# A mixture-of-experts layer in fp32: the third matrix of each expert is loaded from GpSimd's DMA queue instead of SP's

## The chip, the cores and the metric

The kernel runs on one NeuronCore of a Trainium2 chip. The metric is the time of one execution on the device in microseconds. PE is TensorE (matmuls), ACT is ScalarE, DVE is VectorE, POOL is GpSimd, SP is SyncE, which here does nothing but issue DMAs. SP, ACT and GpSimd each have a DMA queue of their own; in the profile q1 is SP's, q10 ACT's and q0 GpSimd's. All of them run on the same 16 DMA engines.

## The reference

The whole is one block of a first model (two sequence branches of a Hyena convolution and an mLSTM, merged, then an expert layer) and two layers of a second model (attention, retention, gated feed-forward), on 256 tokens of 1024 channels, all in fp32. What the change touches is the expert layer. Sixteen experts each pick their 32 best tokens (`cap` = 2 x 256 / 16) and send them through three matrices:

```python
def expert_choice_ffn(h, w_router, w1, w3, w2):
    B, N, D = h.shape
    cap = EC_CAPACITY_FACTOR * N // N_EXPERTS
    aff = jax.nn.softmax((h @ w_router).astype(jnp.float32), axis=-1)
    gate, idx = lax.top_k(jnp.swapaxes(aff, 1, 2), cap)
    bidx = jnp.arange(B)[:, None, None]
    xg = h[bidx, idx]
    a = jnp.einsum('becd,edf->becf', xg, w1)
    b = jnp.einsum('becd,edf->becf', xg, w3)
    ye = jnp.einsum('becf,efd->becd', jax.nn.silu(a) * b, w2) * gate[..., None].astype(h.dtype)
    return jnp.zeros_like(h).at[bidx, idx].add(ye)
```

`w1` and `w3` are 1024 x 2048 for each expert and `w2` is 2048 x 1024, 8 MiB each: 24 MiB per expert and 384 MiB for all. Every weight is used once.

## The kernel before

The program is written by hand, engine by engine, with semaphores. Nothing is scheduled by a tool: what an engine does, and in which order, is the order of its code.

**Chunks and slots.** Each matrix of an expert is loaded in four chunks of 2 MiB, [128 partitions x 16 KiB], and each partition's 16 KiB are contiguous in memory. An expert has `PER_EXPERT` = 12 chunks, in the order of use: c0 to c3 are w1, c4 to c7 are w3, c8 to c11 are w2 (`E1`, `E3`, `E2` in the code). The chunks of all experts go through `XRING` = 8 slots, four in the tile `ring_sb` and four in `arena_sb`: chunk number n of the whole stage lies in slot n mod 8. So eight chunks, two thirds of an expert, are in memory or in flight at a time.

**Who waits for what.** PE adds one to the semaphore `slots_used` with the last matmul on each chunk. The load of chunk n waits until chunk n - 8 has been used, and that is its only wait. Each slot has a semaphore `expert_landed[slot]`; PE waits for it before a chunk (`slot_of`). In the kernel before, SP issues all loads in the order of use: expert 0's first eight chunks are loaded ahead, while the branches before are at work, then a loop over pairs of experts issues 24 loads per turn (L645), and a last part 16 more (L649). After these come, on the same queue, the weights of the next two layers in half chunks of 1 MiB (`halves`, L659); the first four of them go to slots 2, 3, 5 and 6 of the eight and wait for the last expert's c6, c7, c9 and c10 to be used.

**What PE does for an expert** (`expert`, L2065): eight chunks of 16 matmul records, into two banks; after c3 it spreads the next expert's gates; after c7 it turns the gates and the product of the first two matrices (`hact`, which DVE makes once c7 is used), gathers the next expert's tokens by a one-hot product (8 us), and then does c8 to c11 with the turned `hact` (`hTs`, which DVE copies out of PSUM). At the end ACT copies the result and PE scatters it to all tokens; DVE adds it up. The last expert has no gather for a next one.

**GpSimd** has some loads of constants to issue at the beginning, one store, and four loads of small tables at about 310 us (L720). Then it has nothing to do until the two layers after the experts, where it makes the low part of each half chunk (L725).

Of the kernel before, what the change touches and what calls it, by code (L numbers as in the profile page):

```python
# [32 lines left out]
XRING = 8  # L33
# [11 lines left out]
EXPERTS, CAP, FF = 16, 32, 2048  # L45
# [176 lines left out]
def kernel_program(nc, a, k, out):  # L222
# [3 lines left out]
    with ExitStack() as ctx:  # L226
# [3 lines left out]
        def sem(name):  # L230
            return ctx.enter_context(nc.semaphore(name))
# [26 lines left out]
        def region(off, *dims):  # L258
            n = int(np.prod(dims))
            v = arena[:, off:off + n]  # L260
            if len(dims) == 2:
                return v.rearrange("p (a b) -> p a b", a=dims[0])
            if len(dims) == 3:
                return v.rearrange("p (a b c) -> p a b c", a=dims[0], b=dims[1])
            if len(dims) == 4:
                return v.rearrange("p (a b c d) -> p a b c d", a=dims[0], b=dims[1], c=dims[2])
            return v
# [113 lines left out]
        rows = arena[0:4, 4096:4096 + 3136]  # L381
# [19 lines left out]
        def spread_row(ap, off, n):  # L401

            return bass.AP(ap.tensor, off, [[0, P], [1, n]])
# [37 lines left out]
        s = {n: sem(n) for n in names}  # L441
        landed = [sem(f"slot{i}_landed") for i in range(RING)]
        expert_landed = [sem(f"expert{i}_landed") for i in range(XRING)]
        half_landed = [sem(f"half{i}_landed") for i in range(RING)]


# [49 lines left out]
        E1 = a["w_exp1"][0].rearrange("e (p k) f -> e p k f", p=P)  # L496
        E3 = a["w_exp3"][0].rearrange("e (p k) f -> e p k f", p=P)
        E2 = a["w_exp2"][0].rearrange("e (r p c) f -> e r p c f", p=P, c=4)
        PER_EXPERT = 12
        N_POST = N_PRE + PER_EXPERT * EXPERTS  # L500
        def expert_slot(c, *dims):

            i = c % XRING
            if i in EXPERT_ARENA:
                v = region(EXPERT_ARENA[i], SLOT)
            else:
                o = ((N_PRE + EXPERT_RING.index(i)) % RING) * SLOT
                v = ring[:, o:o + SLOT]
            return v.rearrange("p (k c) -> p k c", k=dims[0])
# [23 lines left out]
        for l in range(DEPTH_2):  # L533
# [28 lines left out]
            for i in range(NF // 2):  # L562
                src = a["w_ffn_down_2"][l][2 * P * i:2 * P * (i + 1)].rearrange("(k p) c -> p k c", p=P)
# [6 lines left out]
        def half(n, t=ring):  # L570

            o, (kk, c) = ((N_POST + n) % RING) * SLOT, halves[n][1]
            return tuple(t[:, b:b + kk * c].rearrange("p (k c) -> p k c", k=kk) for b in (o, o + HALF))
# [12 lines left out]
        def wait_emptied(eng, name, n=None):  # L586
# [9 lines left out]
            for e, v in last.items():  # L596
                eng.wait_ge(freed[e], v)

        block = ctx.enter_context(nc.Block())


        @block.sync
        def _(sp):
# [19 lines left out]
            def expert_load(e, c, place=None):  # L623

                place = c if place is None else place
                n = 2 if c < 8 else 4
                src = E2[e, c - 8] if c >= 8 else (E1, E3)[c // 4][e, :, 2 * (c % 4):2 * (c % 4) + 2]
                sp.dma_start(expert_slot(place, n), src).then_inc(expert_landed[place % XRING], 16)

            expert_load(0, 0)  # L630
            sp.wait_ge(s["unit_done"], U.at("yo1", 1) + 1)
# [11 lines left out]
            expert_load(0, 7)  # L643

            with sp.Fori(0, EXPERTS - 2, 2) as e:  # L645
                for c in range(XRING, XRING + 2 * PER_EXPERT):
                    sp.wait_ge(s["slots_used"], e * PER_EXPERT + (c - XRING + 1))
                    expert_load(e + c // PER_EXPERT, c % PER_EXPERT, c)
            for c in range(XRING, 2 * PER_EXPERT):  # L649
                sp.wait_ge(s["slots_used"], (EXPERTS - 2) * PER_EXPERT + c - XRING + 1)  # L650
                expert_load(EXPERTS - 2 + c // PER_EXPERT, c % PER_EXPERT, c)
            for n, (src, _, _, _) in enumerate(halves):
# [8 lines left out]
                for l in range(DEPTH_2):  # L661
                    i = n - half_at["va", l] - RING
# [6 lines left out]
                    if 1 <= i <= 3:  # L669

                        h = HPG * (i - 1)
                        src = bass.AP(rel_table.tensor, 127 + h * P * 384, [[383, P], [P * 384, HPG], [1, T]])
                        sp.dma_start(relB[:, h:h + HPG], src).then_inc(s["lay_landed"], 16)
                    if i == 4:
                        src = bass.AP(a["b_in_2"].tensor, l * IN2 + V_R, [[0, P], [0, 2], [1, 2048]])
# [21 lines left out]
        @block.gpsimd  # L697
        def _(pool):
            g = nc.gpsimd
            g.memset(sTad, 0.0)  # L700
            g.memset(ones[:], 1.0)
            g.memset(cst[:, 0:1], EPS)
            g.memset(cst[:, 1:2], 1.0).then_inc(s["cst_set"], 1)
            g.memset(cst[:, 2:3], LN_EPS).then_inc(s["cst_set"], 1)
            for dst, src in other_loads:
                g.dma_start(dst, src).then_inc(s["small_landed"], 16)

            pool.wait_ge(s["unit_done"], U.at("filt", 7) + 1)
            g.memset(vx[:, :, :, 128:129], 1.0)
            g.memset(vc[:, :, :, 128:129], 1.0).then_inc(s["vaug_ones"], 1)  # L710

            pool.wait_ge(s["rel_ready"], 1)

            g.dma_start(rel_table, relbuf.unsqueeze(1).broadcast_to([AH, P, 384])).then_inc(s["rel_saved"], 16)

            pool.wait_ge(s["unit_done"], U.at("hT", 1) + 1)
            for dst, src in ((ltmask.rearrange("p t s -> p (t s)"), k["ltmask"]), (iota, k["iota"]),
                             (w_router, a["w_router"][0].rearrange("(p k) c -> p k c", p=P)),
                             (fnorm, spread_row(a["final_norm_g"], 0, D))):
                g.dma_start(dst, src).then_inc(s["moe_landed"], 16)  # L720

            for n in range(len(halves)):
                pool.wait_ge(s["hi_ready"], n + 1)
                low, high = half(n, ring_r)
                g.tensor_tensor(low, half(n)[0], high.bitcast(F32), ALU.subtract).then_inc(s["lo_ready"], 1)  # L725
# [1018 lines left out]
        def _(pe):  # L1744
# [63 lines left out]
            for i in range(8):  # L1808
                t, c = divmod(i, 4)
# [30 lines left out]
            for i in range(8):  # L1840
                o, f, q = i // 4, (i // 2) % 2, i % 2
# [70 lines left out]
            for d in range(2):  # L1912
                for t in range(2):
                    c = (d * 2 + t) * 4
# [30 lines left out]
            for kind, r in enumerate((3, 0, 2)):  # L1945
                for d in range(2):
                    for t in range(2):
                        c = kind * 16 + (d * 2 + t) * 4
# [34 lines left out]
            for o in range(2):  # L1983
# [17 lines left out]
                for i in range(2):  # L2001
                    b = open_unit(f"yo{o}", i)
                    for j in range(2):
                        n = 0
# [60 lines left out]
            def expert(e, pair, second, last=False):  # L2065
                def slot_of(c, n):
                    place = PER_EXPERT * second + c
                    pe.wait_ge(expert_landed[place % XRING], 16 * (place // XRING + 1) + pair * (16 * PER_EXPERT // XRING))
                    return expert_slot(place, n)
                pe.wait_ge(s["xg_copied"], e + 1)  # L2070
                for c in range(8):
                    w = slot_of(c, 2)
                    o = bank[c // 4]
                    for q in range(2):
                        kt_ = 2 * (c % 4) + q
                        for g in range(4):
                            ins = mm(o[32 * g:32 * g + 32, :], xg[:, kt_], w[:, q, 512 * g:512 * g + 512], kt_ == 0, kt_ == 7)
                    ins.then_inc(s["slots_used"], 1)
                    if c == 3 and not last:
                        spread_gates(e + 1)  # L2080
                pe.wait_ge(s["sg_copied"], e + 1)
                if not last:
                    pe.wait_ge(s["sel_ready"], e + 2)
                for t in range(2):
                    ins = tr(bank[3][:, t * P:(t + 1) * P], sgs[:, t])
                ins.then_inc(s["sg_turned"], 1)
                pe.wait_ge(s["hact"], e + 1)
                for c in range(4):
                    ins = tr(bank[2][:, c * P:(c + 1) * P], hact[:, c:512:4])
                ins.then_inc(s["hT_turned"], 1)  # L2090
                if not last:
                    gather(e + 1)
                pe.wait_ge(s["hT_evac"], e + 1)
                for r in range(4):
                    w = slot_of(8 + r, 4)
                    for c in range(4):
                        for g in range(4):
                            ins = mm(bank[0][32 * g:32 * g + 32, 0:T], hTs[:, c, 32 * r:32 * r + 32], w[:, c, T * g:T * (g + 1)],
                                     r + c == 0, r + c == 6)
                    ins.then_inc(s["slots_used"], 1)  # L2100

                pe.wait_ge(s["y_evac"], e + 1)
                pe.wait_ge(s["sgT_evac"], e + 1)
                pe.wait_ge(s["acc_done"], e + 1)
                for t in range(2):
                    for g in range(4):
                        ins = mm(bank[4 + g][:, t * T:(t + 1) * T], sgT[32 * g:32 * g + 32, t * P:(t + 1) * P], ysb[32 * g:32 * g + 32])
                ins.then_inc(s["scat_done"], 1)
# [105 lines left out]
            for l in range(DEPTH_2):  # L2214
# [99 lines left out]
                n = half_at["mixo", l]  # L2314
# [154 lines left out]
```

## Time and profile before

| | |
|---|---|
| median of 3 runs | 2553.28 us (2551.95 to 2556.81) |
| the profiled execution | 2555.6 us, its span 2553.8 us |
| mean granted clock of TensorE | 0.906 of full speed |
| PE busy | 2209.2 us, 87% of the span |
| DVE, ACT, GpSimd busy | 725.6, 648.6, 859.1 us |
| DMA | 679.90 MB, mean 266 GB/s |
| loads of expert weights | 192 of 2048 KB, 35.6 us from issue to landing |
| chain that ended last | PE 64%, DMA 29% |

The span is the time that the trace covers, the profiled execution's own time has some us around it, and the median is that of runs without a profile. The shares are means over stages with different limits: the expert stage lies at 447 to 1360 us, and its limit has to be read there. The 35.6 us from issue to landing are no latency, since each load queues behind those issued before it.

### The profile page before, as it was taken

What the parts mean: (1) busy time and instruction counts of PE and PEld (TensorE: products, weight loads), DVE (VectorE), ACT (ScalarE), POOL (GpSimd) and SP (SyncE); (2) the same over time, 40 slices, a digit from 0 to 9 for tenths busy, and PEclk for the clock granted to TensorE, in tenths of its full rate; (3) what the DMA queues carried; (4) which work ended last, traced back from release to release, by engine and by line L of the source; (5) the groups of instructions that cost most, each with busy time, mean ns of one, the idle gap of its engine ahead of it and who ended that gap; (6) DMA issues with size and microseconds to landing.
All of it is one profiled execution on the core that took longest, in us unless ns stands there. A gap on an engine that the chain in (4) does not pass through costs nothing.

```text
span 2553.8 us, 30814 instructions
## 1 busy us (share of the span) xinstructions
PE 2209.2 (87%) x13012; PEld 1553.4 (61%) x13012; DVE 725.6 (28%) x1446; ACT 648.6 (25%) x786; POOL 859.1 (34%) x212
## 2 busy tenths in 40 slices
PE   6999998867777676776666999999999999999998
PEld 2678775323333322222224887887887888888887
DVE  4233433111111111111114152643322152644231
ACT  1211300000000000000002443644443443553442
POOL 1000000000000000000004765777887855677786
PEclk9999997787777878778787999999999999999999
DMA  9456324999999999999996744465655744456563
GB/s 342 128 190 238 113 99 197 389 428 428 429 428 428 429 428 429 429 428 429 428 426 234 241 135 130 149 181 190 207 196 166 259 148 133 132 174 198 185 194 132
DMA packets 236692, 679.90 MB, mean 266 GB/s; under 512 B 8748, under 2 KB 153142, under 8 KB 211313
## 3 DMA queue, kind: packets, MB, share of 16 engines
q1 hardware_dynamic: 233905, 671.54, 69.4%
q0 software_dynamic: 2400, 6.41, 1.0%
q8 instruction: 74, 1.21, 0.2%
q10 hardware_dynamic: 288, 0.53, 0.1%
q14 instruction: 25, 0.20, 0.0%
HBM read 673.85 MB, written 4.59 MB: 266 GB/s over the span
## 4 chain that ended last, share of the span: by engine, by line
PE 64%; DMA 29%; DVE 4%; ACT 1%; issue 1%; POOL 1%; SPq 0%; DVEq 0%; ACTq 0%
PE bank L1759 63%; DMA arena_sb<-w_exp 24%; DMA ring_sb<-w_exp 4%; PE bank L1762 2%; DVE arena_sb L1046 1%; DVE bank L1049 1%; POOL ring_parts L725 1%; DVE x_sb L1049 0%; DMA arena_sb<-hy_skip 0%; ACT ring_parts L911 0%; DVE sm_sb L1530 0%; DVE bank L1046 0%; ACT arena_sb L935 0%; SPq L615 0%; DVE arena_sb L1049 0%
## 5 line engine op out<-in xcount | busy, mean ns | idle before, releaser
L725 POOL TENSOR_TENSOR ring_parts<-ring_sb,ring_parts 128x2048 fp32r<-128x2048 f32 x186 | 848.4, 4578 | 1374.5 <-ACT ring_parts L911 1374.1
L1759 PE MATMUL bank<-arena_sb 128*32 128x256 f32 (+8 forms) x3550 | 562.0, 544 | 148.7 <-DMA arena_sb<-w_exp 112.7
L1759 PEld LDWEIGHTS bank<-arena_sb 128*32 128x32 f32 (+4 forms) x3550 | 318.5, 181 | 358.4 <-DMA arena_sb<-w_exp 154.6
L1759 PE MATMUL bank<-arena_parts,ring_parts 128*128 128x256 f32 (+1 forms) x2288 | 425.9, 334 | 0.0
L1759 PE MATMUL bank<-ring_sb,arena_sb 128*32 128x512 f32 (+2 forms) x2336 | 303.4, 610 | 134.8 <-DMA ring_sb<-w_exp 134.8
L911 ACT CAST ring_parts<-ring_sb 128x2048 fp32r<-128x2048 f32 x186 | 349.7, 1886 | 191.4 <-DMA ring_sb<-w_in 61.2
L1759 PEld LDWEIGHTS bank<-arena_parts,ring_parts 128*128 128x128 f32 x2288 | 359.3, 188 | 48.4
L1046 DVE TENSOR_TENSOR arena_sb<-bank,arena_sb 128x512 f32<-128x512 f32 (+5 forms) x245 | 145.1, 611 | 797.0 <-PE bank L1759 689.4
L1759 PE MATMUL bank<-hT_parts,ring_parts 128*128 128x256 f32 (+1 forms) x1632 | 323.0, 340 | 0.3 <-POOL ring_parts L725 0.3
L1759 PEld LDWEIGHTS bank<-ring_sb,arena_sb 128*32 128x32 f32 (+1 forms) x2336 | 89.1, 126 | 340.8 <-DMA ring_sb<-w_exp 215.4
L1759 PEld LDWEIGHTS bank<-hT_parts,ring_parts 128*128 128x128 f32 x1632 | 262.1, 189 | 38.6 <-issue 1.9
L1759 PE MATMUL bank<-ring_parts,arena_parts 128*128 128x512 f32 (+1 forms) x1152 | 262.3, 385 | 0.0
L1759 PEld LDWEIGHTS bank<-ring_parts,arena_parts 128*128 128x128 f32 x1152 | 212.7, 188 | 42.7
L1046 DVE TENSOR_TENSOR bank<-bank,arena_sb 128x256 f32<-128x256 f32 (+1 forms) x250 | 124.7, 502 | 323.7 <-ACT arena_sb L935 304.3
L901 ACT COPY arena_sb<-bank 128x256 f32<-128x256 f32 x16 | 6.0, 372 | 594.8 <-PE bank L1759 594.8
L1759 PE MATMUL bank<-hT_sb,ring_sb 128*128 128x256 f32 x640 | 142.4, 383 | 0.0
L1759 PEld LDWEIGHTS bank<-hT_sb,ring_sb 128*128 128x128 f32 x640 | 122.2, 192 | 19.6 <-issue 3.1
L1759 PE MATMUL bank<-ring_parts,hT_parts 128*128 128x512 f32 (+1 forms) x432 | 101.6, 390 | 8.6 <-DVE hT_parts L1046 5.1
L1759 PEld LDWEIGHTS bank<-ring_parts,hT_parts 128*128 128x128 f32 x432 | 79.8, 195 | 26.3 <-DVE hT_parts L1046 5.9
L935 ACT ACTIVATE arena_sb<-bank,colC_sb 128x256 f32<-128x256 f32 x132 | 61.9, 473 | 133.5 <-PE bank L1759 133.4
L899 ACT ACTIVATE arena_sb<-bank 128x512 f32<-128x512 f32 x16 | 9.6, 597 | 296.7 <-PE bank L1759 296.7
L1762 PEld LDWEIGHTS bank<-ident_sb,arena_sb 128*128 128x128 f32 x426 | 54.5, 162 | 49.0 <-issue 22.5
(213 smaller groups left out, 1011.0 us busy)
## 6 DMA issues: line engine op xcount, KB each, us to landing
arena_sb<-w_exp SPq DMA_DIRECT2D x96, 2048.0 KB, 35.6
ring_sb<-w_exp SPq DMA_DIRECT2D x96, 2048.0 KB, 35.6
ring_sb<-w_in SPq DMA_DIRECT2D x112, 1024.0 KB, 5.4
ring_sb<-w_ada SPq DMA_DIRECT2D x24, 1024.0 KB, 12.4
ring_sb<-w_ffn_gate SPq DMA_DIRECT2D x22, 1024.0 KB, 5.3
ring_sb<-w_ffn_up SPq DMA_DIRECT2D x22, 1024.0 KB, 5.3
ring_sb<-w_ffn_down SPq DMA_DIRECT2D x22, 1024.0 KB, 4.9
ring_sb<-w_ret_proj SPq DMA_DIRECT2D x16, 1024.0 KB, 5.8
```

The source lines that it names most:

```text
L725: g.tensor_tensor(low, half(n)[0], high.bitcast(F32), ALU.subtract).then_inc(s["lo_ready"], 1)
L899: A.activation(sact, bank[0][:], ACT.Silu).then_inc(s["a_read"], 1)
L901: A.copy(ysb, bank[0][:, 0:T]).then_inc(s["y_evac"], 1)
L911: A.copy(half(n, ring_r)[1], half(n)[0]).then_inc(s["hi_ready"], 1)
L935: A.activation(spare[:, n % 3], bank[u % 8][:, T:2 * T], ACT.Identity, bias=0.0 if c is None else colC[:, c + j:c + j + 1]).then_inc(s["sp ...
L1046: return V.tensor_tensor(o, i0, i1, op)
L1049: return V.scalar_tensor_tensor(o, i0, sc, i1, op0, op1)
L1759: return M.matmul(o, l, r, start=first, stop=last)
L1762: return M.transpose(o, i, ident[:])
```

## The change

The loads of c8 to c11 are issued from GpSimd's queue, in a loop of its own of the same form, with the same waits for `slots_used`. SP's loop leaves these chunks out. Since two queues now fill the same slots, there is a second set of landing semaphores, `rows_landed`, for GpSimd's loads, and PE waits for one or the other; a place of the ring holds a chunk of the third matrix once in a pair of experts. Expert 0's first eight chunks, none of them of the third matrix, are loaded by SP as before. Nothing in the work of PE, ACT or DVE changes.

```diff
+        rows_landed = [sem(f"rows{i}_landed") for i in range(XRING)]
...
+        def first_columns(c0, c1):
+            return [c for c in range(c0, c1) if c % PER_EXPERT < 8]
+        def second_rows(c0, c1):
+            return [c for c in range(c0, c1) if c % PER_EXPERT >= 8]
+        def expert_source(e, c):
+            return E2[e, c - 8] if c >= 8 else (E1, E3)[c // 4][e, :, 2 * (c % 4):2 * (c % 4) + 2]
...
             with sp.Fori(0, EXPERTS - 2, 2) as e:
-                for c in range(XRING, XRING + 2 * PER_EXPERT):
+                for c in first_columns(XRING, XRING + 2 * PER_EXPERT):
                     sp.wait_ge(s["slots_used"], e * PER_EXPERT + (c - XRING + 1))
                     expert_load(e + c // PER_EXPERT, c % PER_EXPERT, c)
-            for c in range(XRING, 2 * PER_EXPERT):
+            for c in first_columns(XRING, 2 * PER_EXPERT):
...
+            def second_load(e, c, place):
+                g.dma_start(expert_slot(place, 4), expert_source(e, c)).then_inc(rows_landed[place % XRING], 16)
+            with pool.Fori(0, EXPERTS - 2, 2) as e:
+                for c in second_rows(XRING, XRING + 2 * PER_EXPERT):
+                    pool.wait_ge(s["slots_used"], e * PER_EXPERT + (c - XRING + 1))
+                    second_load(e + c // PER_EXPERT, c % PER_EXPERT, c)
+            for c in second_rows(XRING, 2 * PER_EXPERT):
+                pool.wait_ge(s["slots_used"], (EXPERTS - 2) * PER_EXPERT + c - XRING + 1)
+                second_load(EXPERTS - 2 + c // PER_EXPERT, c % PER_EXPERT, c)
...
                 def slot_of(c, n):
                     place = PER_EXPERT * second + c
-                    pe.wait_ge(expert_landed[place % XRING], 16 * (place // XRING + 1) + pair * (16 * PER_EXPERT // XRING))
+                    if c >= 8:
+                        pe.wait_ge(rows_landed[place % XRING], 16 + 8 * pair)
+                    else:
+                        uses = len([p for p in first_columns(0, place + 1) if p % XRING == place % XRING])
+                        pe.wait_ge(expert_landed[place % XRING], 16 * uses + 16 * pair)
```

On GpSimd's engine, from the four table loads to its first work for the next layer, before:

```order
L720 DMA arena_sb<-const_ltmask 128x512 [waits unit_done]
L720 DMA arena_sb<-const_iota 128x32
L720 DMA arena_sb<-w_router 128x128
L720 DMA arena_sb<-final_norm_g 128x1024
L725 ISA
L725 TENSOR_TENSOR ring_parts<-ring_sb,ring_parts 128x2048 [waits hi_ready] x4
```

and now, from the last two of the table loads to the second load of the loop:

```order
L731 DMA arena_sb<-w_router 128x128
L731 DMA arena_sb<-final_norm_g 128x1024
L737 UNCONDITIONAL_BRANCH
L737 ISA
L735 ISA [waits slots_used]
L735 DMA arena_sb<-w_exp 128x4096
L739 REGISTER_ALU
L735 ISA [waits slots_used]
L735 DMA arena_sb<-w_exp 128x4096
L739 REGISTER_ALU
```

Eight loads stand in the loop (two are shown) and eight more behind it; line numbers are 11 to 27 higher than before. The loop also has a wait (ISA) and a register step at each load. On SP's queue, the beginning of the loop, before, where the first four loads are those of the third matrix (slots 0 to 3, two in `arena_sb` and two in `ring_sb`):

```order
L628 ISA [waits slots_used]
L628 DMA arena_sb<-w_exp 128x4096
L647 REGISTER_ALU
L628 ISA [waits slots_used]
L628 DMA arena_sb<-w_exp 128x4096
L647 REGISTER_ALU
L628 ISA [waits slots_used]
L628 DMA ring_sb<-w_exp 128x4096
L647 REGISTER_ALU
L628 ISA [waits slots_used]
L628 DMA ring_sb<-w_exp 128x4096
L647 REGISTER_ALU
```

and now, where the same place has the next expert's c0 to c2 (slots 4 to 6):

```order
L639 ISA [waits slots_used]
L639 DMA arena_sb<-w_exp 128x4096
L658 REGISTER_ALU
L639 ISA [waits slots_used]
L639 DMA ring_sb<-w_exp 128x4096
L658 REGISTER_ALU
L639 ISA [waits slots_used]
L639 DMA ring_sb<-w_exp 128x4096
```

SP's loop starts with the next expert's c0, which waits for this expert's c4 to be used; c8 to c11 of this expert, which wait for c0 to c3, are no longer ahead of it.

## Rows read from the trace of the kernel before

**Rows 1.** The page, part 2: 40 equal slices of the span, tenths busy and GB/s.

```profile
DMA  9456324999999999999996744465655744456563
GB/s 342 128 190 238 113 99 197 389 428 428 429 428 428 429 428 429 429 428 429 428 426 234 241 135 130 149 181 190 207 196 166 259 148 133 132 174 198 185 194 132
```

**Rows 2.** Table of stretches: the stage of the expert loads.

```profile
core 0: us, PE busy (x) PEld busy (x) DVE busy (x) ACT busy (x) POOL busy (x), PEclk, DMA share, GB/s
500.00:1300.00 800.00, 569.84 (x4290) 249.70 (x4286) 105.71 (x297) 29.65 (x40) 0.00 (x0) 0.77 1.01 428
```

**Rows 3.** DMA queues, 500 to 1300 us: GB/s in 40 slices, packets, then the queue.

```profile
GB/s 427 426 429 430 425 429 430 428 427 430 429 425 430 430 426 428 431 427 427 432 426 427 432 428 425 431 429 426 430 430 426 428 431 426 428 432 428 425 430 428
DMA packets 23530, 342.68 MB, mean 428 GB/s; under 512 B 2615, under 2 KB 2615, under 8 KB 2615
...
q1 hardware_dynamic: 23526, 342.62, 100.6%
```

**Rows 4.** Waits of PE, 500 to 1300 us: total, times, longest.

```profile
PE bank L1759 <- DMA ring_sb<-w_exp: 120.9, 57, 3.0
PE bank L1759 <- DMA arena_sb<-w_exp: 97.6, 57, 3.0
```

**Rows 5.** Timeline of PE, last expert: start, length, engine, line, tiles.

```profile
1307.14 3.61 PE L1759 MATMUL bank<-ring_sb,arena_sb 128*32 128x512 f32 x16 [2.87 <-DMA ring_sb<-w_exp]
1312.03 1.92 PE L1759 MATMUL bank<-ring_sb,arena_sb 128*32 128x512 f32 x16 [1.29 <-DMA ring_sb<-w_exp]
...
1351.19 3.35 PE L1759 MATMUL bank<-ring_sb,arena_sb 128*32 128x256 f32 x32 [2.96 <-DMA ring_sb<-w_exp]
1356.10 1.93 PE L1759 MATMUL bank<-arena_sb 128*32 128x256 f32 x32 [1.56 <-DMA arena_sb<-w_exp]
```

**Rows 6.** Timeline of SP's queue, first load of the loop.

```profile
451.13 2.02 SPq L628 DMA_DIRECT2D arena_sb<-w_exp  x2
```

**Rows 7.** Chain that ended last, 400 to 1400 us: start, length, what.

```profile
1320.17 35.88 DMA arena_sb<-w_exp
```

**Rows 8.** Waits of SP, 500 to 1300 us.

```profile
SPq L628 <- PE bank L1759: 714.6, 164, 12.3
```

**Rows 9.** Timeline of GpSimd, the first of four loads in a row.

```profile
309.71 0.56 POOL L720 DMA_DIRECT2D arena_sb<-const_ltmask  x1 [233.18 <-PE bank L1762]
```

**Rows 10.** DMA issues, whole program: count, KB each, us to landing.

```profile
ring_sb<-w_in SPq DMA_DIRECT2D x112, 1024.0 KB, 5.4
...
arena_sb<-final_norm_g POOLq DMA_DIRECT2D x1, 512.0 KB, 8.7
```

**Rows 11.** DMA queues, 315 to 317 us.

```profile
q0 software_dynamic: 136, 0.37, 53.4%
q1 hardware_dynamic: 163, 0.33, 46.4%
```

**Rows 12.** Timeline of all engines, the middle of one expert.

```profile
749.08 1.92 PE L1759 MATMUL bank<-ring_sb,arena_sb 128*32 128x512 f32 x16 [1.41 <-DMA ring_sb<-w_exp]
...
752.40 11.27 PE L1759 MATMUL bank<-arena_sb 128*128 128x32 f32 x64
752.60 0.69 DVE L1476 COPY arena_sb<-bank 128x512 f32<-128x512 f32 x1
760.13 0.43 DVE L1046 TENSOR_TENSOR arena_sb<-bank,gcol_sb 128x256 f32<-128x256 f32 x1 [6.84 <-PE bank L1759]
...
763.44 4.13 PE L1759 MATMUL bank<-ring_sb,arena_sb 128*32 128x256 f32 x64
```

**Rows 13.** Timeline of SP's queue, first loads of the next layer.

```profile
1335.00 20.14 SPq L659 DMA_DIRECT2D ring_sb<-w_in  x4
```

**Rows 14.** Timeline of ACT, its first cast for the next layer.

```profile
1368.72 3.69 ACT L911 CAST ring_parts<-ring_sb 128x2048 fp32r<-128x2048 f32 x2
```

**Rows 15.** Table of stretches: SP's queue alone, then both queues.

```profile
311.50:313.50 2.00, 2.00 (x5) 0.90 (x6) 0.00 (x0) 0.00 (x0) 0.35 (x1) 1.00 1.05 409
314.50:317.50 3.00, 3.00 (x9) 1.33 (x8) 2.27 (x4) 0.00 (x0) 0.00 (x0) 1.00 1.06 376
```

More of the change, by code:

```diff
@@ L625, in expert_load @@
                 place = c if place is None else place
-                n = 2 if c < 8 else 4
-                src = E2[e, c - 8] if c >= 8 else (E1, E3)[c // 4][e, :, 2 * (c % 4):2 * (c % 4) + 2]
-                sp.dma_start(expert_slot(place, n), src).then_inc(expert_landed[place % XRING], 16)
+                sp.dma_start(expert_slot(place, 2), expert_source(e, c)).then_inc(expert_landed[place % XRING], 16)
             expert_load(0, 0)
```

## The prediction, made before the changed kernel ran

> **What bounds the kernel now.** I read the page's 40 slices first. From slice 8 to slice 20 the DMA line stands at 9 and moves 426 to 429 GB/s, beside 100 to 260 in most of the program after it [rows 1]. The table of stretches puts numbers to it: from 500 to 1300 us the 16 DMA engines are busy for 1.01 of the time at 428 GB/s, PE for 570 of 800 us, at a granted clock of 0.77 of full speed, so partly at 1.2 and partly at 2.4 GHz; GpSimd does nothing [rows 2]. The DMA rows say that all of this is one queue, q1 (SP's), in packets that come to 16.4 KB each: 342.6 MB over 23530 - 2615 packets [rows 3]. The waits agree: PE waits 120.9 + 97.6 us for expert weights there [rows 4]. The timeline shows the step: weight matmuls start at 1307.14 and 1312.03 [rows 5], so one 2 MiB chunk every 4.89 us, and an expert of 12 chunks takes 58.7 us. From SP's first load of the loop at 451.13 [rows 6] to the last chunk's landing at 1356.05 (1320.17 + 35.88 in the chain [rows 7]) are 905 us for 184 chunks. The time of this stage is bytes over rate. PE's order changes it only if it lets the DMA engines run dry, or in what is left to do after the last chunk.
>
> **What the change moves.** I number an expert's chunks c0 to c11; c8 to c11 are its third matrix. All 64 of these loads leave SP's queue for GpSimd's; slots, slot waits, bytes and PE's order stay. What follows:
>
> 1. Issuing. SP has 64 issues fewer, which is worth nothing: it spends 714.6 us of 800 waiting for PE to use a slot [rows 8]. GpSimd gets 64 issues of 0.56 us or so each [rows 9], some 36 us in a stage in which it is idle and nobody waits for it; its loop is over before its first work for the next layer. Cost 0. A transfer may start later: a 512 KB load on this queue took 8.7 us to land, beside a busy SP queue, where SP's 1 MiB loads have a median of 5.4 [rows 10]. But a chunk's slot is freed 8 x 4.89 = 39 us before its use, so a few us are hidden as long as something else is in flight. Cost 0 as well.
>
> 2. The order of arrival. With one queue chunks land in the order of use. With two, c8 starts as soon as its slot is free instead of behind seven others. In the stretch where both queues have something to carry, 315 to 317 us, q0 moved 0.37 MB and q1 0.33 MB in 136 and 163 packets [rows 11]: about half each. So I let both share the rate equally. Then per expert: c8 to c11 are released as c0 to c3 are used, and take 4 x 9.8 = 39 us; SP brings four chunks in the same time, 9.8 us each, and then four more alone in 19.6 us. Sum 58.7 us, as before.
>
> 3. Do the engines run dry? The danger is after c7. PE then turns hact, gathers the next expert's tokens and only then starts c8: c7 ends at 751.0, the gather runs from 752.4 to 760.1, which is 9.1 us after c7, and c8 is done at 763.4 [rows 12]. Before, c10 and c11 still land in that time. Now c8 to c11 are there, and what is in flight are the four chunks c0 to c3 of the next expert, 19.6 us of transfers, against some 12 us until the first slot comes free. 7 us to spare: the rate holds. Cost 0, but this is where the cover can go (see the starvation below).
>
> 4. The tail. Before, the last thing to land is c11 at 1356.05, and behind it stand only its matmuls, 1.93 us, to 1358.03 [rows 5]. Now the third matrix comes early and c7 late. The last bytes still land at 1356 (same bytes, rate and start), shared by c7 and c11; c7's slot was freed earlier, so it lands up to one half-rate chunk before them, at 1346 to 1356. I take 1349. Behind it stand its matmuls (2.7 us, the mean of the two lengths in the timeline, 1.9 and 3.5), the chain to c8 (from c7's end at 751.00 to the end of DVE's copy of the turned hact at 753.29: 2.3 [rows 12]; the last expert has no gather), and four chunks of the third matrix back to back (10.8): 1349 + 15.8 = 1364.8, 6.8 us later than 1358.03. Ends: c7 at 1346 and PE at 2.4 GHz (1.9 + 2.3 + 7.7) gives 1358, or 0; c7 last of all and PE at 1.2 GHz (3.6 + 2.3 + 14) gives 1376, or +18. I take +8, as a PE that has waited for c7 may be at the lower level. The four half chunks of the next layer, issued from 1335 on [rows 13] and needed by ACT at 1368.7 [rows 14], ride behind c7 instead of behind c11 and are not late. The rest of the program only shifts.
>
> 5. The rate with two queues. The trace has no expert load on GpSimd's queue, so this is bounded from neighbours. q1 alone, 311.5 to 313.5 us: 409 GB/s. Both queues, 314.5 to 317.5 us: 376 GB/s [rows 15], 8% less, with small packets. Both queues would be active for 2/3 of the 905 us (39 of 58.7), 603 us. Upper end, the same ratio, 409/376 = 1.088: +53 us. If the loss is a fixed one per packet instead, it shrinks with size: a mean packet there is 0.70 MB/299 = 2.3 KB, here 16.4 KB, so 0.088 x 2.3/16.4 = 1.2%, or +7 us. Lower end: two full slices of the stage stand at 429 against a mean of 428 [rows 1], and within it finer slices at 432 [rows 3]; a second queue that fills gaps all the time could give 1%, -8 us. I take the per-packet reading, +7 us, since the stretch it comes from is the nearest row there is and the packets are what differs most.
>
> Sum on the profiled execution, 2555.6 us: 8 + 7 more are 2570.6. The runs' median is 2.3 us lower, 2553.28, so 2568.
>
> The Trainium skill (DMA: Bandwidth & Descriptors, "Issuing engines are not separate DMA queues") says that spreading DMAs over issuing engines saves only issue time. The trace agrees as far as SP's issue time is free; by this rule step 5 would be 0 and the result 2561.
>
> **Rivals.**
> *Starvation of GpSimd's queue.* If its packets are small and the engines alternate packet by packet, it gets far less than half while SP has work: with packets of 4 KB against 16.4, one fifth. For it: nothing in the trace shows a large packet from this queue. Against it: bytes came out even at 315 to 317 us, though the packets differed in number [rows 11]. Then c10 and c11 land last, with SP's next eight chunks but one already in their slots, and the engines have nothing to carry in two gaps: while PE does c11 and SP starts the load it admits (2.7 + 1.4), and, when that has landed, until PE has closed the expert and done the next c0 and GpSimd's first load starts (2.5 + 2.7 + 4, less 4.9 for the one chunk). The 1.4 and 4 are my estimates from the landings in [rows 10], less the transfers. About 8 us per expert over 15 experts: +117, with the tail 2680; partly so, 2590 to 2640.
> The Trainium skill (same page, "Queues, rings and completion order" and "SWDGE vs HWDGE vs iDMA") has engines going round the queues a packet at a time, and GpSimd's packets preferably at most 4096 bytes: read literally this is that case. The trace bears it out only in part, for the bytes were even.
> *The mixed rate is 8% lower* for large packets too: 2553 + 53 + 8 = 2614. For it the one mixed stretch; against it that its packets are small, and that some engines may have had nothing left to do.
> *Hidden anyway, no change.* The tail is at its lower end (c7 early, PE at 2.4 GHz) and the rate stays: 2553 to 2558.
> *Faster.* Two queues leave fewer gaps, 432 GB/s for 428: -8, with a tail of +2: 2547.
>
> **Chances.** Forecast (equal shares, tail, small loss) 0.50, mostly 2559 to 2580; lower mixed rate 0.13; starvation 0.10; no change 0.17; faster 0.10. The runs tell a change from none at about 0.2%, 5 us. So slower 0.73, same 0.17, faster 0.10. The range reaches from within the faster case, 2548, to just over the lower mixed rate, 2618, and leaves out the full starvation.
>
> **What would show it.** Step 2: in the DMA rows of the stage q0 has a third of the bytes; PE's waits are for the expert's c4 to c7, with some 9.8 us between their starts, and c8 to c11 run without any. Step 3: the DMA line stays at 9 in every slice; an 8, or PE waiting for the third matrix, means starvation. Step 4: behind the last c7 stand four back-to-back chunks, and the last scatter comes 6 to 10 us after the last landing. Step 5: 424 to 426 GB/s from 500 to 900 us by the forecast, 404 by the proportional loss, 432 by the gain. The forecast is wrong if the 905 us of the stage change by more than 15, or if anything after the experts changes by more than 3.

## The result and the profile after

The changed kernel takes 2561.63 us (median of 7 runs, 2559.89 to 2565.55) against 2553.47 us before (7 runs): a ratio of 1.0034, 95% interval 1.0024 to 1.0044, so 8 us slower, between 6 and 11. The profiled execution's span is 2561.0 us, 7.2 us longer than before. The forecast was 2568, made of +8 for the tail (what PE still has to do behind its last wait for a weight) and +7 for the rate with two queues. The sign and the mechanism of the tail were right; the rate did not change at all.

Part 2 of the page of the changed kernel, the same 40 slices (PE busy, granted clock, DMA busy, GB/s):

```profile
PE   6999998766666767666666999999999999999998
...
PEclk9999997777777677677777999999999999999999
DMA  9456324999999999999995844455655844356553
GB/s 338 130 192 236 112 99 197 381 427 429 427 429 429 428 429 428 428 429 428 428 427 195 270 132 132 143 178 181 217 187 171 260 142 147 117 181 203 184 195 132
```

The DMA line holds 9 from slice 8 to 20, at 427 to 429 GB/s, as in [rows 1]. The stretch from 500 to 1300 us, in the columns of [rows 2], and its DMA rows:

```profile
500.00:1300.00 800.00, 529.01 (x4158) 241.74 (x4150) 106.21 (x301) 29.87 (x40) 28.75 (x55) 0.72 1.01 428
```

```profile
DMA packets 23515, 342.64 MB, mean 428 GB/s; under 512 B 2602, under 2 KB 2602, under 8 KB 2602
...
q1 hardware_dynamic: 15528, 226.20, 66.4%
q0 software_dynamic: 7983, 116.38, 34.2%
```

428 GB/s and a share of 1.01, the same as before [rows 2, 3], though a third of the bytes now comes through q0. The packets are as large as before: (342.64 MB) / (23515 - 2602) = 16.4 KB. (The 2602 packets under 512 B, 16 for each load, hold 4 bytes each; they count as packets in the rows below too.) PE is at a lower mean clock, 0.72 for 0.77. The waits of PE in this stretch:

```profile
PE bank L1782 <- DMA ring_sb<-w_exp: 178.2, 28, 7.9
PE bank L1782 <- DMA arena_sb<-w_exp: 82.4, 15, 7.0
```

260.6 us in 43 waits, where [rows 4] has 218.5 in 114: fewer and longer ones. The timeline of PE in the middle of an expert (start, length, as in [rows 5]) shows which:

```profile
745.23 3.17 PE L1782 MATMUL bank<-arena_sb 128*32 128x512 f32 x16 [4.42 <-DMA arena_sb<-w_exp]
755.02 3.64 PE L1782 MATMUL bank<-ring_sb,arena_sb 128*32 128x512 f32 x16 [6.62 <-DMA ring_sb<-w_exp]
764.81 3.64 PE L1782 MATMUL bank<-ring_sb,arena_sb 128*32 128x512 f32 x16 [6.16 <-DMA ring_sb<-w_exp]
...
769.95 11.28 PE L1782 MATMUL bank<-arena_sb 128*128 128x32 f32 x64
780.99 4.78 PE L1782 MATMUL bank<-ring_sb,arena_sb 128*32 128x256 f32 x64
785.60 1.90 PE L1782 MATMUL bank<-arena_sb 128*32 128x256 f32 x32
```

The last three chunks before the gather start at 745.23, 755.02 and 764.81, 9.8 us apart instead of 4.89 [rows 5], each after 4 to 7 us of waiting; then come the gather and, without a wait for DMA, c8 to c11 (records at 769.95, 780.99 and 785.60). This is step 2 of the prediction as forecast, but for c4: it starts at 738.88 without a wait, where the prediction had waits for c4 to c7. GpSimd's own rows, its loads for expert 0 and the first of the next four, and the landing times from part 6 of the page:

```profile
453.45 0.53 POOL L735 DMA_DIRECT2D arena_sb<-w_exp  x1 [139.73 <-PE bank L1782]
...
498.00 0.53 POOL L735 DMA_DIRECT2D arena_sb<-w_exp  x1 [38.92 <-PE bank L1782]
```

```profile
arena_sb<-w_exp POOLq DMA_DIRECT2D x32, 2048.0 KB, 14.6
ring_sb<-w_exp POOLq DMA_DIRECT2D x32, 2048.0 KB, 30.2
```

Each issue takes 0.53 us, and between groups of four GpSimd is idle for 39 to 56 us. The four loads of a group are issued within some 5 us and land one after the other, so the medians of 14.6 and 30.2 us are places in that row. Now the end of the stage, the last expert on PE:

```profile
1345.43 3.64 PE L1782 MATMUL bank<-ring_sb,arena_sb 128*32 128x512 f32 x16 [6.15 <-DMA ring_sb<-w_exp]
1355.20 3.64 PE L1782 MATMUL bank<-ring_sb,arena_sb 128*32 128x512 f32 x16 [6.14 <-DMA ring_sb<-w_exp]
...
1359.66 0.89 PE L1785 MATMUL bank<-ident_sb,arena_sb 128*128 128x128 f32 x4 [0.20 <-DVE arena_sb L1069]
1361.33 1.93 PE L1782 MATMUL bank<-arena_sb 128*32 128x256 f32 x32 [0.78 <-DVE arena_sb L1499]
1363.08 3.64 PE L1782 MATMUL bank<-ring_sb,arena_sb 128*32 128x256 f32 x64
1366.54 1.91 PE L1782 MATMUL bank<-arena_sb 128*32 128x256 f32 x32
1368.94 1.15 PE L1782 MATMUL bank<-arena_sb 32*128 32x256 f32 x16 [0.49 <-ACT arena_sb L924]
```

c6 starts at 1345.43 and c7 at 1355.20, and each of them had been waited for 6.1 us. In [rows 5] the last record of this kind that waits is c11 at 1356.10, followed by nothing but the scatter, in the trace of before:

```profile
1358.53 1.15 PE L1759 MATMUL bank<-arena_sb 32*128 32x256 f32 x16 [0.49 <-ACT arena_sb L901]
```

In the changed kernel the scatter starts at 1368.94: behind the landing of c7 stand its own matmuls, 3.64 us, the turned `hact` until 1360.55, its copy, and the four chunks of w2 from 1361.33 to 1368.45. c7 is not the last chunk to land. GpSimd's load of c11, issued at 1323.75, has this row (DMA issues of 1323 to 1324.5 us, the last number from issue to landing):

```profile
arena_sb<-w_exp POOLq DMA_DIRECT2D x1, 2048.0 KB, 35.1
```

It lands at 1358.85, 3.7 us after c7, and nobody waits for it, since PE comes to it at 1366.54. From the first load of the loop, GpSimd's at 453.45, to this landing are 905.4 us, as before. So all the bytes arrive in the same time, and what costs is that the last chunk that PE has to wait for now has four others behind it. The granted clock of the two parts (columns of [rows 2]):

```profile
1355.00:1359.00 4.00, 3.79 (x17) 0.82 (x18) 0.09 (x1) 0.00 (x0) 0.00 (x0) 0.50 0.94 376
1361.00:1369.00 8.00, 7.17 (x132) 4.12 (x132) 5.08 (x5) 0.47 (x2) 0.00 (x0) 1.00 0.65 227
```

c7 runs at 0.50, the level of 1.2 GHz, after PE has waited 6.1 us for it; the four chunks of w2 run at 1.00, that of 2.4 GHz.

### The profile page after: what moved, and what is told of

It reads as the page before. It is cut to its first block, busy times and chain, and to the rows that moved or that the text cites. A ratio compares the mean times of both kernels' runs of the same rounds, so it can differ in the third digit from the quotient of the medians.

```text
span 2561.0 us, 30831 instructions
## 1 busy us (share of the span) xinstructions
PE 2177.8 (85%) x13012; PEld 1553.8 (61%) x13012; DVE 725.5 (28%) x1446; ACT 648.5 (25%) x786; POOL 892.7 (35%) x276
## 4 chain that ended last, share of the span: by engine, by line
PE 69%; DMA 23%; DVE 4%; ACT 1%; issue 1%; POOL 1%; SPq 0%; DVEq 0%; POOLq 0%; ACTq 0%
PE bank L1782 67%; DMA ring_sb<-w_exp 13%; DMA arena_sb<-w_exp 10%; PE bank L1785 2%; DVE arena_sb L1069 1%; POOL ring_parts L748 1%; DVE bank L1072 1%; ACT ring_parts L934 0%; DVE x_sb L1072 0%; DMA arena_sb<-hy_skip 0%; DVE sm_sb L1553 0%; DVE bank L1069 0%; DMA ring_sb<-w_ffn_gate 0%; DVE arena_sb L1072 0%; ACT arena_sb L958 0%
## 5 line engine op out<-in xcount | busy, mean ns | idle before, releaser
L1782 PE MATMUL bank<-arena_sb 128*32 128x256 f32 (+8 forms) x3550 | 541.1, 520 | 126.5 <-DMA arena_sb<-w_exp 91.1
L735 POOL DMA_DIRECT2D arena_sb<-w_exp x32 | 16.9, 528 | 938.8 <-PE bank L1782 938.8
## 6 DMA issues: line engine op xcount, KB each, us to landing
arena_sb<-w_exp POOLq DMA_DIRECT2D x32, 2048.0 KB, 14.6
ring_sb<-w_exp POOLq DMA_DIRECT2D x32, 2048.0 KB, 30.2
```

The lines of the kernel that those rows point to most:

```text
L735: g.dma_start(expert_slot(place, 4), expert_source(e, c)).then_inc(rows_landed[place % XRING], 16)
L1782: return M.matmul(o, l, r, start=first, stop=last)
```

## The experiments

The table gives, for each profiled execution, the first matmul on an expert chunk, the first work of GpSimd for the next layer, what lies between them (the stage), and the rest of the span. Everything is read from the timelines of PE and GpSimd. Each ratio is against runs of the kernel before beside it; e5 and e6 ran on another chip than e1 to e4 (medians of before: 2554.50 and 2552.94 us).

| kernel | first matmul | first low part | stage, us | against before | rest of the span | ratio of the runs (95%) |
|---|---|---|---|---|---|---|
| before | 447.58 | 1370.69 | 923.1 | | 1630.7 | |
| changed | 449.45 | 1381.10 | 931.7 | +8.5 | 1629.3 | 1.0034 (1.0024 to 1.0044) |
| e1, last expert back on SP | 450.62 | 1374.20 | 923.6 | +0.5 | 1628.0 | 0.9999 (0.9989 to 1.0009) |
| e2, last expert alone on GpSimd | 448.75 | 1382.47 | 933.7 | +10.6 | 1630.4 | 1.0038 (1.0023 to 1.0052) |
| e3, w1 on GpSimd instead of w2 | 451.07 | 1374.53 | 923.5 | +0.4 | 1629.3 | 1.0005 (0.9994 to 1.0015) |
| e4, 4 KB packets on GpSimd's queue | 448.42 | 1433.73 | 985.3 | +62.2 | 1625.8 | 1.0215 (1.0198 to 1.0233) |
| e5, 4 KB packets for w2, all on SP | 449.63 | 1389.78 | 940.2 | +17.0 | 1627.2 | 1.0066 (1.0045 to 1.0087) |
| e6, 4 KB packets on both queues | 451.01 | 1421.68 | 970.7 | +47.6 | 1632.8 | 1.0204 (1.0187 to 1.0221) |

The rest of the span varies over 7 us among the eight executions, without following any edit that I can name (no edit touches the kernel behind the stage); what the edits do is in the stage.

**e1: the last expert's third matrix back on SP.** Four of the 64 loads are returned.

```diff
-            for c in first_columns(XRING, 2 * PER_EXPERT):
+            for c in first_columns(XRING, 2 * PER_EXPERT) + second_rows(PER_EXPERT, 2 * PER_EXPERT):
...
-            for c in second_rows(XRING, 2 * PER_EXPERT):
+            for c in second_rows(XRING, PER_EXPERT):
...
-                    if c >= 8:
+                    if c >= 8 and last:
+                        pe.wait_ge(expert_landed[place % XRING], 48 + 16 * pair)
+                    elif c >= 8:
```

> The changed kernel, but the third matrix of the last expert (four of the 64 loads) is back on SP's queue, in the order of use. Tail theory: all of the +8 us comes from the last expert, where four chunks' matmuls now stand behind the last landing instead of one; with c8 to c11 last again, the time is that of before, 2553 +- 2 (ratio 0.999 to 1.001), and the span from the last landing to the last scatter is 4 us as before, not 14. Rival, a cost spread over the stage (rate with two queues, start of loads, PE's lower clock): 15 of 16 experts still use both queues, so 15/16 of the loss stays, 2561 (ratio 1.003).

Measured: 2554.07 us, ratio 0.9999. The loss is gone, with 15 of 16 experts still on two queues. The timeline of PE at the end of the stage (c7, c10, c11, scatter):

```profile
1340.02 2.79 PE L1782 MATMUL bank<-ring_sb,arena_sb 128*32 128x512 f32 x16 [2.98 <-DMA ring_sb<-w_exp]
...
1354.69 3.54 PE L1782 MATMUL bank<-ring_sb,arena_sb 128*32 128x256 f32 x32 [2.96 <-DMA ring_sb<-w_exp]
1359.60 1.93 PE L1782 MATMUL bank<-arena_sb 128*32 128x256 f32 x32 [1.36 <-DMA arena_sb<-w_exp]
1362.03 1.15 PE L1782 MATMUL bank<-arena_sb 32*128 32x256 f32 x16 [0.49 <-ACT arena_sb L924]
```

c7 is done at 1342.81, 17 us before c11's matmuls start, and c11 is again the last to be waited for. The rival of a cost spread over the stage falls: it had 1.003, and the interval ends at 1.0009.

**e2: only the last expert's third matrix on GpSimd's queue**, in the kernel before.

```diff
-            for c in range(XRING, 2 * PER_EXPERT):
+            for c in range(XRING, 2 * PER_EXPERT - 4):
...
+            for c in range(2 * PER_EXPERT - 4, 2 * PER_EXPERT):
+                pool.wait_ge(s["slots_used"], (EXPERTS - 2) * PER_EXPERT + c - XRING + 1)
+                g.dma_start(expert_slot(c, 4), E2[EXPERTS - 1, c % PER_EXPERT - 8]).then_inc(rows_landed[c % XRING], 16)
```

> The kernel before, but the third matrix of the last expert alone (four loads) is issued from GpSimd's queue. Tail theory: the whole loss appears with these four loads, 2561 to 2562 (ratio 1.003 to 1.004), the last expert's c4 to c7 start 9.8 us apart and all other experts' chunks 4.9. Rival of a spread cost: 1/16 of the loss, under 1 us, 2553 to 2554.

Measured: ratio 1.0038, so four loads of 192 make the whole loss, and the stage is longer by 10.6 us. PE in the last expert:

```profile
1336.22 3.48 PE L1764 MATMUL bank<-arena_sb 128*32 128x512 f32 x16 [6.54 <-DMA arena_sb<-w_exp]
1346.02 3.64 PE L1764 MATMUL bank<-arena_sb 128*32 128x512 f32 x16 [6.32 <-DMA arena_sb<-w_exp]
...
1357.01 3.32 PE L1764 MATMUL bank<-ring_sb,arena_sb 128*32 128x512 f32 x16 [2.09 <-DMA ring_sb<-w_exp]
...
1362.69 1.93 PE L1764 MATMUL bank<-arena_sb 128*32 128x256 f32 x32 [0.79 <-DVE arena_sb L1481]
1364.44 3.64 PE L1764 MATMUL bank<-ring_sb,arena_sb 128*32 128x256 f32 x64
1367.90 1.91 PE L1764 MATMUL bank<-arena_sb 128*32 128x256 f32 x32
1370.30 1.15 PE L1764 MATMUL bank<-arena_sb 32*128 32x256 f32 x16 [0.49 <-ACT arena_sb L906]
```

Chunks 9.8 us apart at 1336.22 and 1346.02, one landing last before 1357.01, and behind it the three records of w2 and the scatter at 1370.30. (The expectation had c4 to c7 all 9.8 us apart. c2 to c5 are, and the last two follow at 6 and 5 us: with one queue until then, c0 to c3 are used one by one, GpSimd's four loads go out from 1305.5 to 1330.0, and the last of them lands at 1349.4 (19.4 us after its issue), before c6 and c7 have come. So here c7 lands last of all, at 1357.0, where in the changed kernel it came 3.7 us before the last landing; that makes these four loads alone cost 2 us more than all 64.)

**e3: the first matrix on GpSimd's queue instead of the third.** c0 to c3 of all experts, expert 0's too, are issued by GpSimd and c4 to c11 by SP.

```diff
         def first_columns(c0, c1):
-            return [c for c in range(c0, c1) if c % PER_EXPERT < 8]
+            return [c for c in range(c0, c1) if c % PER_EXPERT >= 4]
         def second_rows(c0, c1):
-            return [c for c in range(c0, c1) if c % PER_EXPERT >= 8]
+            return [c for c in range(c0, c1) if c % PER_EXPERT < 4]
```

> The same split, a third of each expert on GpSimd's queue, but it is the first half of the first two matrices' chunks in order of use, c0 to c3 (w1), that GpSimd loads, for all experts, and SP loads c4 to c11. Tail theory: in the last expert c0 to c3 come early and c11 lands last, so one chunk's matmuls stand behind the last landing as before: 2553 +- 3. Two queues are active for as long as in the changed kernel, so a rival that lays the loss on the second queue itself expects 2561. A third outcome, over 2565, would mean that c8 to c11 at half rate arrive too late for PE and slots stay full: the DMA rate in the stage would be below 428 GB/s.

Measured: 2554.7 us, ratio 1.0005. Both queues carry about as much as in the changed kernel (q0 has 114.43 MB from 500 to 1300 us, for 116.38), at 428 GB/s, and nothing is lost. c10 and c11 on PE:

```profile
1355.04 3.57 PE L1784 MATMUL bank<-ring_sb,arena_sb 128*32 128x256 f32 x32 [2.96 <-DMA ring_sb<-w_exp]
1359.94 1.93 PE L1784 MATMUL bank<-arena_sb 128*32 128x256 f32 x32 [1.33 <-DMA arena_sb<-w_exp]
```

c11 is the last that PE waits for, and one chunk's matmuls stand behind it. What costs is which chunk PE waits for last, not the second queue.

**e4: small packets on GpSimd's queue.** This asks what the prediction's starvation rival hangs on: how the DMA engines share between the queues.

```diff
-                g.dma_start(expert_slot(place, 4), expert_source(e, c)).then_inc(rows_landed[place % XRING], 16)
+                for h in range(2):
+                    g.dma_start(expert_slot(place, 4)[:, h::2], expert_source(e, c)[:, h::2]).then_inc(rows_landed[place % XRING], 16)
```

> The changed kernel with each of GpSimd's 2 MiB loads cut in two of 1 MiB, every second row of 4 KiB, so that its packets are 4 KB instead of 16 KB, beside SP's 16 KB. It asks how the DMA engines share between two queues. If they take turns packet by packet, GpSimd's queue gets one fifth of the rate while SP has work: c8 to c11 arrive late, PE waits for them, the engines run dry, and the time is 2640 to 2690. If they share by bytes or time, GpSimd still gets about half: PE waits for c4 to c7 only, and the time is that of the changed kernel, 2561, plus what small packets cost on a third of the bytes (409 against 428 GB/s, 4 percent of 300 us, 12 us): 2561 to 2575.

Measured: 2610.86 us, ratio 1.0215: neither of the two expected times. The DMA rows say which theory holds. First the changed kernel, 740 to 770 us, where both queues have work (packets, MB, share), then e4, 720 to 750:

```profile
q0 software_dynamic: 448, 6.55, 51.3%
q1 hardware_dynamic: 433, 6.31, 49.4%
```

```profile
q1 hardware_dynamic: 695, 10.08, 79.1%
q0 software_dynamic: 693, 2.69, 21.9%
```

Nearly equal numbers of packets in both: 448 and 433, then 693 and 695. (In the second stretch 116 of them are the packets of 4 bytes; without these it is 657 packets of 4 KB beside 615 of 16 KB.) With 16 KB on both sides that is half the bytes each; with 4 KB against 16 KB, q0 gets 2.69 of 12.77 MB, 21%. That is what turns packet by packet give. PE then does what the rival said, it waits for the third matrix:

```profile
731.56 3.58 PE L1783 MATMUL bank<-arena_sb 128*32 128x256 f32 x32 [2.75 <-DMA arena_sb<-w_exp]
753.92 3.64 PE L1783 MATMUL bank<-ring_sb,arena_sb 128*32 128x256 f32 x32 [18.78 <-DMA ring_sb<-w_exp]
```

18.78 us of waiting for c10. While it waits, the DMA engines are still busy; they run out of work when PE is at c10 and c11 (two stretches, columns of [rows 2]):

```profile
720.00:752.00 32.00, 12.39 (x89) 8.34 (x88) 0.85 (x2) 0.00 (x0) 0.00 (x0) 0.63 1.01 426
756.00:760.00 4.00, 2.65 (x28) 0.99 (x24) 0.00 (x0) 0.00 (x0) 0.00 (x0) 0.50 0.79 258
```

Only the price was too high in the rival: an expert takes 62.1 us here (the scatters at 700.90 and 762.98), 3.4 more than 58.7, where I had worked out 8. The mean of the stretch from 500 to 1300 us is 405 GB/s for 428:

```profile
500.00:1300.00 800.00, 488.96 (x4056) 241.23 (x4056) 102.05 (x286) 29.29 (x39) 72.77 (x104) 0.71 0.99 405
```

**e5: the same small packets without a second queue.** The kernel before, SP's loads of w2 cut as in e4.

```diff
+                for h in range(2 if c >= 8 else 0):
+                    sp.dma_start(expert_slot(place, n)[:, h::2], src[:, h::2]).then_inc(expert_landed[place % XRING], 16)
```

> The kernel before, all loads on SP's queue in the order of use, but each load of the third matrix cut in two of 1 MiB with every second row of 4 KiB, as in the run with small rows on GpSimd's queue. It asks how much of that run's +57 us is the small packets themselves and how much the turns between two queues of unequal packets. Turns theory: with one queue there are no turns; a third of the bytes at the rate of small packets (409 for 428 GB/s) costs at most 14 us of 302: 2553 to 2567, and PE waits evenly for all chunks. Rival, small packets are the cost: 2600 to 2611 here too.

Measured: ratio 1.0066, 2568.85 us, just over the upper end of the expectation. The stretch:

```profile
500.00:1300.00 800.00, 557.76 (x4150) 241.07 (x4142) 106.22 (x301) 29.88 (x40) 0.00 (x0) 0.78 1.01 422
```

422 GB/s: 4 KB packets for a third of the bytes cost 1.4% of the rate, 13 us of 905, of the stage's +17. Of the other 4, 1.6 are c11's own matmuls, which ran 3.54 us where [rows 5] has 1.93; the rest I can't place. If the two effects add up, which no run tests, then of e4's 62 us some 17 are the small packets and 45 the unequal turns. The changed kernel's tail is not in them: in e4's last expert c11 comes last again, PE waits for it until 1416.48 and scatters at 1420.61.

**e6: 4 KB packets on both queues**, the changed kernel with all expert loads cut in two.

```diff
+                src = (E1, E3)[c // 4][e, :, 2 * (c % 4):2 * (c % 4) + 2].rearrange("p k (h f) -> p (k h) f", f=1024)
+                for h in range(2):
+                    sp.dma_start(expert_slot(place, 4)[:, h::2], src[:, h::2]).then_inc(expert_landed[place % XRING], 16)
```

> The changed kernel with the loads of both queues cut in two of 1 MiB with rows of 4 KiB, so that both queues have 4 KB packets. If the DMA engines take turns packet by packet, equal packets give equal shares again, as with 16 KB on both: both queues near 205 GB/s where both have work, PE's waits back on c4 to c7 and none of 14 to 20 us on c10, no slice of the stage in which the engines stand idle. The time is then the changed kernel's 2561 plus the rate of 4 KB packets on all bytes, 409 to 425 for 428 GB/s, 6 to 42 us: 2567 to 2603. If GpSimd's queue still gets a fifth (a share fixed by the queue or by its small packets alone), the waits for c10 stay and the time is above 2611.

Measured: 2605.64 us, ratio 1.0204, a little over the expected 2603. The queues from 700 to 720 us, and the stretch from 500 to 1300:

```profile
q0 software_dynamic: 1065, 4.10, 51.5%
q1 hardware_dynamic: 1063, 4.09, 51.1%
```

```profile
500.00:1300.00 800.00, 522.69 (x4088) 237.48 (x4084) 104.13 (x291) 29.28 (x39) 73.81 (x106) 0.75 1.03 410
```

1065 and 1063 packets and 4.10 and 4.09 MB: equal packets give equal bytes again, so GpSimd's queue has no smaller share of its own. PE's longest wait for a weight is 8.3 us, and the third matrix is not waited for. The rate is 409 or 410 GB/s in every slice, against 428: 905 x (428/410 - 1) = 40 us, and with the tail of 8.5 that is about the stage's +47.6. One queue with 4 KB packets does no better: e5's 422 GB/s with a third of the bytes in them comes to about 410 for that third (3/422 - 2/428 = 1/410). So with 4 KB packets as with 16 KB ones a second queue costs no rate. The mixed stretch of [rows 15] had still smaller packets, 2.5 KB in the mean (1.13 MB in 456 packets); what made its 376 is open. In time e6 is little better than e4, 2606 for 2611: cutting all loads small evens the turns and costs the rate of small packets on all bytes.

## Why the prediction was right or wrong

- *What bounds the stage.* Right. 428 GB/s before and after; PE's lower clock and longer waits inside the stage cost nothing.
- *Step 1, issuing.* Right, 0. GpSimd's 64 issues of 0.53 us lie in idle time.
- *Step 2, equal shares.* Right in the number, by luck, and wrong in the reason. In [rows 11] I read 0.37 and 0.33 MB as an even split of bytes. The other columns of these rows, 136 and 163 packets, were as near to even, and that was the rule: e4 and e6 show turns by packets. The forecast held because GpSimd's packets turned out to be 16 KB as SP's are, which no row of before could show.
- *Step 3, the engines don't run dry.* Right for this change, with equal packets. e4 shows where the cover goes: with a fifth of the rate for the third matrix the same split costs some 45 us, by the sum given there. (The prediction's terms for the two gaps add up to 8.4 us, which over 15 experts is 126 and not 117; e4 has 3.4 us an expert.)
- *Step 4, the tail.* The right term: +8 forecast (the sum gave 6.8, and I rounded it up for a slow PE), +8.5 in the stage of the changed kernel and +10.6 in e2, and e1 takes it away. Within it two choices were off and cancelled in part, so that so close a hit is partly luck. I let c7 land at 1349; it landed at 1355.16 (the stage began 1.9 us later, so 1353.3 on the clock of before). And I gave w2's chunks 2.7 us each; they took 1.8, at 2.4 GHz, 7.1 us for the four. That PE would be at the lower level behind the wait held for c7 alone.
- *Step 5, the rate with two queues.* Wrong, the term is 0 and not +7, and it is the reason why the forecast was 6.4 us too high (2568 for 2561.6). The nearest row I had was a mixed stretch of 3 us with small packets, and I carried its 8% over in a reduced form. (For its lower end I read two full slices at 429 in [rows 1]; there are five, which changes nothing in it.) e3 bounds the term: two queues for the whole stage and no loss, 1.0005. The rule that I had named, that issuing from several engines saves issue time only (the Trainium skill, DMA: Bandwidth & Descriptors, "Issuing engines are not separate DMA queues"), gave 2561, and the measurement is 2561.6.
- *The rivals.* The lower mixed rate and the faster case (432 GB/s) both fell, and so did no change: 2561.6 is clear of its 2553 to 2558. Starvation did not happen but is real. Its rule, one packet per queue in turn, stands in the Trainium skill (same page, "Queues, rings and completion order"); e4 agrees, 693 to 695 packets. The preference of 4096 bytes for packets of GpSimd's queue that the Trainium skill states (same page, "SWDGE vs HWDGE vs iDMA") does not show here: rows of 16 KB went out as packets of 16 KB.
- *"Anything after the experts changes by more than 3 us."* By the letter this sign did appear. From the first low part to the end of the span are 1183.1 us before (2553.8 - 1370.69) and 1179.9 now: 3.2 less. But the six other executions have 1177.4 to 1181.8 there with the same code, so 3 us was less than this part varies, and the sign was set too tight.

## What to carry to other kernels

In this stage, which is bound by DMA, a second queue changed not the rate but the order of arrival. In such a stage ask which piece its consumer waits for last and how much work stands behind it: here one chunk's matmuls before; after, its own and those of four more with a chain between, 8 us, all of it in the last of sixteen experts. If loads have to be split over queues, give the second queue what is used first (e3), and keep the packets of both equally large, and large (e4, e6): the engines take turns by packet, so the queue with the small ones is starved, and small ones on both cost 4% of the rate.

## What was not expected of the hardware

- Two queues with 16 KB packets move as much as one, 428 GB/s, and share it 448 to 433 by packets.
- 4 KB packets on one queue beside 16 KB on the other: 693 to 695 packets in 30 us, and 21% of the bytes for the queue with the small ones.
- GpSimd's queue sends a contiguous row of 16 KB as one packet: 16.4 KB a packet in the mean of both queues, and 448 packets for 6.55 MB on q0.
- A rate of 410 GB/s with 4 KB packets against 428 with 16 KB, 4% (e6), and 422 with a third of the bytes in 4 KB (e5).
